# Late stage of a hybrid SSD/attention block: two raw buffers for the up weights, another order in the last pair, gathered tiles loaded block by block

## The reference

```python
h = rms_norm(x, norm_ffn_pre_w)
up = causal_dwconv(h @ ffn_w_up, ffn_conv_w, ffn_conv_b)   # 1024 -> 2 x 2816, 3 taps over tokens
gate, val = _split(up, (FFN_D_FF, FFN_D_FF))
ff = (jax.nn.gelu(gate, approximate=True) * val) @ ffn_w_down   # 2816 -> 1024
return x + rms_norm(ff, norm_ffn_post_w)
```

## Time and profile before

| | |
|---|---|
| median of 3 runs | 2226.29 us (2220.85 to 2228.31) |
| the profiled execution | 2228.14 us, its span 2226.6 us |
| TensorE, matmul busy | 2105.3 us (95%), 10250 matmuls |
| VectorE busy | 1354.7 us (61%) |
| ScalarE busy | 844.5 us (38%) |
| GpSimd busy | 630.8 us (28%) |
| TensorE idle, put down to conv_a (L1994) | 32.9 us in 20 waits |
| TensorE idle, put down to split_down (L2031) | 13.9 us in 4 waits |
| mean granted TensorE clock | 0.98 of full speed |

### The profile page before, as it was taken

How to read it: one execution, slowest core, us unless ns; L and a number is a source line. 1 busy time by engine, 2 the same in 40 slices (tenths; PEclk the granted TensorE clock), 3 DMA queues, 4 the chain that set the end, 5 groups by cost and what they waited for, 6 DMA issues and landing times. The chain is left out here.

```text
span 2226.6 us, 29363 instructions
## 1 busy us (share of the span) xinstructions
PE 2105.3 (95%) x10250; PEld 1744.0 (78%) x10250; DVE 1354.7 (61%) x1828; ACT 844.5 (38%) x1589; POOL 630.8 (28%) x604
## 2 busy tenths in 40 slices
PE   7999999979999999999889999999999999979997
PEld 7888889968878778788678888887777777768885
DVE  6855453237777767777543445578887887842532
ACT  5322221024454544554442223344333333433432
POOL 1000011145575566665410000032332332310000
PEclk9999999989999999999999999999999999989999
DMA  6132342233343343443264343212122122453343
GB/s 218 62 95 84 104 162 87 85 116 106 104 150 121 108 129 115 130 121 98 75 233 142 137 152 131 101 57 76 66 85 75 66 76 76 168 220 95 105 153 90
DMA packets 131838, 254.79 MB, mean 114 GB/s; under 512 B 25329, under 2 KB 70513, under 8 KB 131729
## 3 DMA queue, kind: packets, MB, share of 16 engines
q1 hardware_dynamic: 85584, 174.98, 24.3%
q0 software_dynamic: 15936, 57.42, 7.4%
q10 hardware_dynamic: 30208, 20.98, 2.9%
HBM read 189.63 MB, written 63.70 MB: 114 GB/s over the span
## 5 line engine op out<-in xcount | busy, mean ns | idle before, releaser
L155 PE MATMUL ps_zg<-u_hi,g_hi 128*128 128x512 f32 x448 | 186.2, 416 | 0.0
L157 PE MATMUL ps_zg<-u_hi,g_lo 128*128 128x512 f32 x448 | 177.3, 396 | 0.0
L156 PE MATMUL ps_zg<-u_lo,g_hi 128*128 128x512 f32 x448 | 176.1, 393 | 0.0
L2031 DVE TENSOR_TENSOR lt_d_lo<-lt_w_raw,lt_d_hi 128x640 fp32r<-128x640 f32 (+1 forms) x64 | 56.8, 891 | 154.6 <-ACT lt_d_hi L1759 145.0
L967 POOL TENSOR_TENSOR mx_seg<-mx_seg,mx_cbm 128x1024 f32<-128x1024 f32 x32 | 76.0, 2374 | 156.1 <-DVE mx_cbm L1124 156.1
L155 PE MATMUL lt_ps<-lt_h_hi,lt_w_hi 128*128 128x512 f32 x256 | 100.6, 393 | 15.2 <-DVE lt_h_lo L2069 14.0
L155 PE MATMUL ps_zg<-z_w,u_hi 128*128 128x512 f32 x256 | 107.2, 419 | 7.8 <-DVE mx_silu L1149 6.9
L1637 POOL TENSOR_TENSOR lt_t_f<-lt_w_raw 128x512 f32<-128x512 f32 x21 | 26.7, 1274 | 289.0 <-DMA lt_w_raw<-in_w_up 287.2
L155 PE MATMUL lt_ps<-lt_h_hi,lt_a_hi 128*128 128x512 f32 x184 | 74.6, 405 | 32.9 <-DVE lt_xc_a L1994 32.9
L1759 ACT ACTIVATE lt_d_hi<-lt_w_raw 128x640 fp32r<-128x640 f32 (+1 forms) x64 | 50.6, 791 | 135.1 <-PE lt_ps L157 124.1
L157 PE MATMUL ps_zg<-z_w,u_lo 128*128 128x512 f32 x256 | 101.6, 397 | 0.0
(11 more groups left out here) (390 smaller groups left out, 6275.9 us busy)
## 6 DMA issues: line engine op xcount, KB each, us to landing
lt_w_raw<-in_w_up SPq DMA_DIRECT2D x44, 512.0 KB, 4.1
mx_a_row<-acs_s SPq DMA_DIRECT2D x32, 512.0 KB, 3.9
g_raw<-in_w_xbc SPq DMA_DIRECT2D x24, 512.0 KB, 3.7
tok_s<-fr_work POOLq DMA_DIRECT2D x24, 512.0 KB, 4.0
lt_sig<-gate_s SPq DMA_DIRECT2D x24, 512.0 KB, 3.7
lt_w_raw<-in_w_down SPq DMA_DIRECT2D x32, 384.0 KB, 3.1
ff_s<-lt_fo SPq DMA_DIRECT2D x21, 512.0 KB, 2.6
lt_w_raw<-in_w_down SPq DMA_DIRECT2D x32, 320.0 KB, 2.9
```

The costliest lines, as they stand in the source:

```text
L155: pe.matmul(dst, s_hi, m_hi, start=first, stop=False)
L156: pe.matmul(dst, s_hi, m_lo, start=False, stop=False)
L157: return pe.matmul(dst, s_lo, m_hi, start=False, stop=last)
L2031: dve.tensor_tensor(d_lo[:, m % 2, 0:n], w_raw[:, m % 2, 0:n], d_hi[:, m % 2, 0:n].bitcast(F32), ALU.subtract).then_inc(dw_lo_done, 1)
```

## The change

- Up weights: a second raw buffer w_raw2 (8 KB a partition at 148, where y_t and, later, d_hi lie). Odd pairs use w_raw, even pairs w_raw2. Tile a and b share a semaphore for each buffer (raw_in). `load_next(i)` waits until all seven splits and all sums of pair i - 2 are done; before, the load waited for splits five and six of pair i - 1. The loops of SP, POOL, ACT and DVE have two pairs in a body; PE's loop is as it was. DVE's pairs 1 and 2 stand ahead of its loop, before it was pair 1 alone.
- The first down loads (blocks 0 and 1) wait for the seventh split of the last pair, before for the sixth.
- Last pair, DVE: before, conv_b, c11, c21, ff 8 to 11, conv_a, fo, split_down(2), split_down(3), ff 12 to 20; now c11, ff 8 to 11, c21, conv_b, split_down(2), ff 12 to 15, split_down(3), conv_a, ff 16 to 20, fo. ACT: gelu behind ff 8 to 11, then tap_a, split_down(2), ff 12 to 15, split_down(3), the load of the activation table, ff 16 to 20.
- Second half: gather g of `SECOND` waits for block_used of 8 + 2g; the loads of res follow the last.

```diff
+        w_raw2 = at("w_raw2", 148, [P, 2, KT, P])
...
+        def raw(odd):
+
+            tiles = w_raw if odd else w_raw2
+            return tiles[:, 0], tiles[:, 1]
...
+        def raw_count(i, odd):
+            return 16 * i + 16 if odd else 16 * i
...
-            def load_pair(i):
-
-                sp.wait_ge(op_lo_done, N_OPS * i - (2 * N_OPS - 5))
-                sp.wait_ge(t_ready, N_SUMS * i - N_SUMS)
-                load_b(i)
-                sp.wait_ge(op_lo_done, N_OPS * i - (2 * N_OPS - 6))
-                load_a(i)
+            def load_pair(i, odd):
+                for dst, f in zip(raw(odd), (2 * i, 2 * i + 1)):
+                    sp.dma_start(dst, A["w_up"][f]).then_inc(raw_in[odd], 16)
+
+            def load_next(i, odd):
+
+                sp.wait_ge(op_lo_done, N_OPS * i - 2 * N_OPS)
+                sp.wait_ge(t_ready, N_SUMS * i - 2 * N_SUMS)
+                load_pair(i, odd)
...
-                    sp.wait_ge(op_lo_done, N_OPS * LAST - 1)
+                    sp.wait_ge(op_lo_done, N_OPS * LAST)
...
-            load_pair(2)
-            with sp.Fori(0, FT - 3) as i:
-                store_ff(i)
-                load_pair(i + 3)
+            sp.wait_ge(turned, NT)
+            load_pair(2, False)
+            load_next(3, True)
+            with sp.Fori(0, (FT - 4) // 2) as n:
+                for j in range(2):
+                    store_ff(2 * n + j)
+                    load_next(2 * n + (j + 4), bool(j))
+            store_ff(FT - 4)
             store_ff(FT - 3)
...
-            def weight_sums(i):
-
-                pool.wait_ge(a_in, 16 * i + 16)
-                pool.wait_ge(b_in, 16 * i + 16)
+            def weight_sums(i, odd):
+
+                raw_b, raw_a = raw(odd)
+                pool.wait_ge(raw_in[odd], raw_count(i, odd))
...
-            with pool.Fori(1, LAST) as i:
-                pool.wait_ge(op_lo_done, N_OPS * i)
-                weight_sums(i + 1)
-                more_weight_sums(i + 1)
+            with pool.Fori(0, (LAST - 1) // 2) as n:
+                for j in range(2):
+                    i = 2 * n + (j + 2)
+                    pool.wait_ge(op_lo_done, N_OPS * i - N_OPS)
+                    weight_sums(i, bool(j))
+                    more_weight_sums(i, bool(j))
...
             for g, (k, place) in enumerate(SECOND):
+                pool.wait_ge(block_used, PB + 2 * g)
                 pool.dma_start(place, ff_s[k:k + place.shape[1], :, HALF:SEQ].rearrange("k p n -> p k n")).then_inc(g_in[g], 16)
...
             tap_b(i, False)
-            gelu(i)
             for k in range(8, 12):
                 split_ff(0, k)
+            gelu(i)
             tap_a(i, False)
+            split_down(2)
+            for k in range(12, 16):
+                split_ff(0, k)
+            split_down(3)
             act.preload_act_table_set("natural_log_exp_and_others")
-            for m in range(2, 4):
-                split_down(m)
-            for k in range(12, LAST):
+            for k in range(16, LAST):
                 split_ff(0, k)
...
-            conv_b(i)
             c11(i)
-            c21(i)
             for k in range(8, 12):
                 split_ff(0, k)
+            c21(i)
+            conv_b(i)
+            split_down(2)
+            for k in range(12, 16):
+                split_ff(0, k)
+            split_down(3)
             conv_a(i)
+            for k in range(16, LAST):
+                split_ff(0, k)
             gated(i, False)
-            for m in range(2, 4):
-                split_down(m)
-            for k in range(12, LAST):
-                split_ff(0, k)
             split_down(4)
```

More of the change, by code:

```diff
@@ L1414, in late @@
             s.sem(n) for n in "h0_done a22_kept s3_ready s1_ready s2_ready s4_ready s3_hi_done s3_lo_done sum_hi_done sum_lo_done".split())
-        a_in, b_in, first_hi_done, first_lo_done, op_hi_done, op_lo_done, t_ready = (
-            s.sem(n) for n in "a_in b_in first_hi_done first_lo_done op_hi_done op_lo_done t_ready".split())
+        first_hi_done, first_lo_done, op_hi_done, op_lo_done, t_ready = (
+            s.sem(n) for n in "first_hi_done first_lo_done op_hi_done op_lo_done t_ready".split())
         first_done, first_kept, product_done, p1_kept, u2_ready, u3_ready, u4_ready = (
@@ L1639, in weight_sums, with more_weight_sums @@
                 pool.tensor_tensor(t_f[:, 1], raw_b[:, HI], t_f[:, 0], ALU.subtract).then_inc(t_ready, 1)
-            def more_weight_sums(i):
+            def more_weight_sums(i, odd):
+                raw_b, raw_a = raw(odd)
                 pool.tensor_tensor(t_f[:, 2], raw_b[:, LO], raw_b[:, HI], ALU.subtract).then_inc(t_ready, 1)
@@ L1706, in split_h, with split_op @@
                     act.activation(h_hi[:, LO, c], h_f[:, 1, LO, c], ACT.Copy).then_inc(s3_hi_done, 1)
-            def split_op(n, i, first):
-                (hi, _), raw, used, needed = OPS[n]
+            def split_op(n, i, odd, first):
+                (hi, _), src, used, needed = ops(odd)[n]
                 if not first:
@@ L1715, in split_op @@
                 else:
-                    act.wait_ge(b_in if n == 4 else a_in, 16 * i + 16)
-                act.activation(hi, raw, ACT.Copy).then_inc(op_hi_done, 1)
+                    act.wait_ge(raw_in[odd], raw_count(i, odd))
+                act.activation(hi, src, ACT.Copy).then_inc(op_hi_done, 1)
             def keep_p1(i):
@@ L1869, in _ @@
             for n in range(4, 6):
-                split_op(n, 1, True)
+                split_op(n, 1, True, True)
             gelu(0)
             tap_a(0, True)
-            split_op(6, 1, True)
-            with act.Fori(1, LAST) as i:
-                pair(i)
+            split_op(6, 1, True, True)
+            with act.Fori(0, (LAST - 1) // 2) as n:
+                for j in range(2):
+                    pair(2 * n + (j + 1), bool(j))
             i = LAST
@@ L1954, in split_sum, with split_op @@
                 dve.tensor_tensor(lo[:], src, hi[:].bitcast(F32), ALU.subtract).then_inc(sum_lo_done, 1)
-            def split_op(n, i):
-                (hi, lo), raw, _, _ = OPS[n]
+            def split_op(n, i, odd):
+                (hi, lo), src, _, _ = ops(odd)[n]
                 dve.wait_ge(op_hi_done, N_OPS * i - (N_OPS - 1 - n))
-                dve.tensor_tensor(lo, raw, hi.bitcast(F32), ALU.subtract).then_inc(op_lo_done, 1)
+                dve.tensor_tensor(lo, src, hi.bitcast(F32), ALU.subtract).then_inc(op_lo_done, 1)
             def combine(i, product, dst, in_bank, other, sem):
@@ L2008, in gated, with pair @@
                 dve.tensor_tensor(fo[:], xc_b[:], xc_a[:], ALU.mult).then_inc(ff_done, 1)
-            def pair(i, second):
+            def pair(i, next_odd, second=False):
                 conv_a(i - 1)
-                split_op(0, i + 1)
+                split_op(0, i + 1, next_odd)
                 gated(i - 1, second)
                 u2_of(i)
-                split_op(1, i + 1)
+                split_op(1, i + 1, next_odd)
                 u3_of(i)
-                split_op(2, i + 1)
+                split_op(2, i + 1, next_odd)
                 u4_c22(i)
-                split_op(3, i + 1)
+                split_op(3, i + 1, next_odd)
                 c12(i)
@@ L2152, in _ @@
             for n in range(4, N_OPS):
-                split_op(n, 1)
-            pair(1, True)
-            with dve.Fori(2, LAST) as i:
-                pair(i, False)
+                split_op(n, 1, True)
+            pair(1, False, True)
+            pair(2, True)
+            with dve.Fori(1, (LAST - 1) // 2) as n:
+                for j in range(2):
+                    pair(2 * n + (j + 1), bool(j))
             i = LAST
```

59 lines of the change are left out of this document (27 added, 32 removed).

## The result

The changed kernel takes 2205.46 us in the median of its runs (2204.49 to 2205.56), beside 2227.07 for the kernel before on the same chip: ratio 0.9908, 95% interval 0.9889 to 0.9926, so it is about 0.9% faster. The forecast was 2205.0.

The account below looks back on a forecast made before the run. VectorE's chain with two hops to ScalarE was taken to bound the loop, TensorE following. Terms -14.5 - 1.5 - 5.6 + 0.3 = -21.3 us took the median from 2226.29 to 2205.0 us; range 2197 to 2216.

Parts of the forecast that it names:

- The loop: Loop over pairs: two raw buffers let GpSimd's sums start at the seventh split's end + 0.2 us; cycles 20.45, -14.5 us.
- B: Loop: sums start later or the two sides share, cycles at the old best pace of 20.90; 2214 us, chance 0.17.
- F: Loop: another wait keeps the sums at the old start, only the end gives 7 us; 2219 us, chance 0.05.
- E: Loop: conv_a's taps and GpSimd's sums also take turns, so the kernel is slower; 2250 us, chance 0.04.
- D: Loop: VectorE keeps the turn for fo behind a_lo, 0.4 us a pair more gain; 2197 us, chance 0.07.
- The ceiling: Loop: TensorE's 84 matmuls of 0.232 us take 19.5 us a cycle; reaching that would give -33 us, called out of reach.
- How the turns are taken: Loop: VectorE's two-SBUF-input instructions and GpSimd's sums exclude each other; starting 1.08 us sooner ends a_lo 1.08 sooner.
- The last pair: Last pair: down weights split ahead of conv_a and fo, ScalarE's order keeps most of the stall before block 2; -1.5 us.
- The later loads of blocks 0 and 1: First down loads, now waiting for the seventh split, still land in time: 0, at most 0.8 us.
- The pacing: Second half: gathers issued block by block, f_post lands sooner, no gap or half clock at block 6; -5.6 us.
- The cost of the paced gathers: Second half: each gather meets the down weights, the last is followed at once by res; +0.3 us.

Follow-up runs that it names:

- e1: Changed kernel with the second raw buffer alone: last pair in the old order, second-half gathers in one go; 2210.96 us, ratio 0.9932.
- e9: Changed kernel with an unread 128x256 GpSimd subtraction ahead of each pair's four weight sums, so they start later; 2219.02 us, ratio 0.996.
- e5: Changed kernel with each loop pair's third and fourth weight sums cut to 8 of 512 columns (result not the layer's); 2174.61 us, one run.
- e6: Changed kernel with VectorE's loop order turned: u2, u3, u4 and c22, which read PSUM, ahead of a_lo, fo and t_lo; 2174.06 us, ratio 0.9767.
- e4: Changed kernel with GpSimd also waiting for the first tap of conv_a before its first sum of a pair; 2210.15 us, ratio 0.9934.
- e3: Changed kernel with ScalarE's and VectorE's order of the last pair as before; 2205.47 us, ratio 0.9905.
- e2: Changed kernel with the seven second-half gathers issued in one go behind the last fo, as before; 2212.86 us, ratio 0.9932.
- e11: Changed kernel with gathers not paced and VectorE's wait for f_post moved from ahead of split_down(6) to its first reader; 2206.95 us, ratio 0.9907.
- e10: e8 with ScalarE's split_down(3) moved ahead of gelu and tap_a; 2168.81 us, ratio 0.9738.
- e8: Changed kernel with both reorderings, e6's of the loop and e7's of the end; 2170.76 us, ratio 0.9746.
- e7: Changed kernel with split_down(2) ahead of gelu and conv_b, split_down(3) to (5) as needed, f_post awaited at its first reader; 2202.07 us, ratio 0.9889.

## Why the prediction was right, and where it was not

- **The loop, -14.5 us: right, measured -15.35.** The sums start 0.17 us after the split (0.2 assumed), a_lo is shorter by 0.98, and the cycle is 20.42 for 20.45. e1 shows that the buffers alone do it, e9 that the cycle follows the start of the sums us for us with all else that two buffers bring in place. The surplus of 0.8 us over the forecast is in the first two cycles, 20.26 and 20.20, and 0.02 us in each of the others, which take 20.43. Rivals B and F fall with the releaser and the cycle, E with the tap's 1.28, D with fo's 2.31. The ceiling beside it was wrong: the step "84 matmuls of 370.64/1598" divided a busy time that runs on past the last matmul before each gap and holds stretches at half clock. From start to start a matmul takes 0.2267, which is 19.04 us a cycle, 0.45 less. The changed kernel's own row, 367.45/1601 at a clock of 1.00, still gives 19.3, so some 0.2 of the error goes with the lower clock (0.99) and the rest with the gaps. It didn't touch this forecast, since VectorE set the pace, but it is most of why e5 and e6 were put 9 to 14 us too high; the rest is what TensorE was behind, which the gap ahead of block 2 took up. And "out of reach while tap_b, gelu and tap_a keep their places" was wrong: they keep them in e6, which runs below 19.5.
- **How the turns are taken: right in kind, incomplete.** The prediction read the earlier trace rows as turns, and e9 confirms the slope of one. What it missed is that the slope ends between 1.28 and 1.30 us, though both sides of the step stood in its own rows; e4's expectation failed by that. e4 alone would have suggested that a late start hardly costs.
- **The last pair, -1.5 us: the gap as forecast, its worth half or less.** 7.45 us for 9.0, by the steps given (split_down(2) at 1942.93, behind gelu and tap_a). But the term took a shorter gap as won time. Between the profiles of the two kernels it was, 1.56 us, since the clock of the kernel before fell late in its gap; that was luck. e3 shows 0.8 us from the split to the end, as the full clock came back no sooner, and e1 against e2, without pacing, nothing. The later loads of blocks 0 and 1 cost nothing, as said: TensorE has no wait for these blocks.
- **The pacing, -5.6 us: right mechanism, too small a term.** Against e2 it is worth 8.0 (7.4 by the medians), and 6.9 with the old order. In e2 f_post took 9.8 us, and TensorE lost 4.82 us to the gap and 2.9 at half clock; the prediction priced the stall of the kernel before (3.9 and 1.6), though with the new order ahead of it TensorE comes to the wait earlier. The total from block 2 on, -6.4 for an expected -5.3 after the cost of the gathers, has also a wait of 0.33 us late in the down projection that is gone, which I didn't look for. e11 adds that the pacing isn't needed for most of it: the burst did harm chiefly through one wait that stood six split_downs ahead of its first use.
- **The cost of the paced gathers, +0.3: not seen.** They start between 1970.72 and 2017.29, no wait of TensorE answers to any of them, and the down weights land in 3.2 and 2.9 us.
- **The sum.** Between the two profiles the three stretches gave 23.3 us for 21.3 forecast; the medians differ by 2227.07 - 2205.46 = 21.6. Half a microsecond went to the stages ahead, the rest lies within what single profiles differ from medians. The steps were off by 0.8 and 1.1 us, and the stages ahead and the difference of profiles from medians took most of that back: a forecast within 0.5 us of the median is closer than its steps deserve, and that is luck.

## What to carry to other kernels

Where two engines exclude each other on SBUF, look at who arrives first at each meeting before you price a shift by its length: the time is a sawtooth in the start, and the spread of one kernel's own cycles may already draw it. Better than to shift the start is to put that engine's PSUM work where the other one reads SBUF; here that was worth some 30 us on top of the second buffer's 15. A wait belongs at the first reader, not at the place where its DMA was issued, and TensorE's own pace should be read from the starts of its matmuls in a stretch without a gap, not from its busy time or from another engine's cycle.

## What the runs showed of the hardware

- A VectorE instruction with two SBUF inputs of 128 x 512 takes 0.68 us alone and up to 1.79 behind a GpSimd subtraction, in one cycle of the kernel before 1.80; a GpSimd one takes 1.26 to 1.32 alone and 1.60 to 2.29 behind VectorE's. When both sides have work queued they alternate, one instruction each. VectorE's taps (1.27 to 1.29 us) and combinations (0.67 to 0.70) with an operand in PSUM ran at their own length beside the sums, in all kernels.
- TensorE's fp32r matmuls of 128x512, with new weights for each, start 0.2267 us apart at full clock when nothing holds them up (e5, e6, and the stretches without a wait in the kernel before).
- After a gap of TensorE of 7.4 to 9.0 us, the granted clock was at its lower level for the first 4 to 6 us of new work, and longer after the shorter gap (5.9 us after 7.45, 4.3 after 9.0) in e3 beside the changed kernel, but not in the kernel before (6.1 after 9.0). A single gap of 1.29 us (e11) or 1.36 (e10) brought no lower clock; gaps of 2.67 (e8), 3.82 (e7) and 4.82 us (e2) did. In the loop of the kernel before, the clock was 0.66 over 1727 to 1732 and again over 1853 to 1858, behind gaps of 2.05 and 2.08 us; in the changed kernel's loop, with gaps of up to 1.16 us, it was 1.00 throughout. What exactly sets the fall and the return is left open.
- A 512 KB row broadcast to all partitions landed in 3.7 to 4.2 us beside down weights alone, and in 8.9 to 10.1 us behind a burst of gathers at some 400 GB/s. Loads of 320 KB on the same queue went from 2.9 to 7.1.
